# A hybrid decoder step on eight cores: the first two tiles taken block by block as weights land, and MLP weights converted to bf16 in a DRAM scratch

## The reference, cut to what matters

```python
h = rms_norm(x) * (1 + sc1) + sh1                    # shifts, scales and gates come from c @ w_ada + b_ada
q, fz, i, g, gb, gc, hv = split(h @ w_in)            # seven blocks of 512 columns
o_rec, s_rec_new = hgrn2_chunked(q, 1 - f, log(f), i, s_rec)      # f = lb + (1 - lb) * sigmoid(fz); state 4 x 128 x 128
o_rec = per_head_rms(o_rec) * g_onorm * silu(g)
y_conv, s_conv_new = short_conv(gc * hv, s_conv, w_conv)
x = x + g1 * (concat([o_rec, gb * y_conv]) @ w_out)
h2 = rms_norm(x) * (1 + sc2) + sh2
x = x + g2 * (square(relu(h2 @ w_up)) @ w_down)      # 1024 -> 4096 -> 1024
y = rms_norm(x) * g_final
```

## Time and profile before

| | us |
|---|---|
| median of three runs (1062.84 to 1077.37) | 1071.49 |
| the profiled execution | 1065.07 |
| its span on the slowest core, core 1 (all cores: 1051.7 to 1063.5) | 1063.5 |
| PE busy in the span | 837.0 (79%) |
| DVE / ACT / POOL busy | 476.9 / 341.9 / 213.9 |
| granted TensorE clock, mean of the slowest core | 0.953 |

### The profile page before, as it was taken

How to read it: one execution, slowest core, us unless ns; L and a number is a source line. 1 busy time by engine, 2 the same in 40 slices (tenths; PEclk the granted TensorE clock), 3 DMA queues, 4 the chain that set the end, 5 groups by cost and what they waited for, 6 DMA issues and landing times.

```text
span 1063.5 us, 16556 instructions; the slowest of 8 cores (1051.7 to 1063.5 us)
## 1 busy us (share of the span) xinstructions
PE 837.0 (79%) x5943; PEld 517.9 (49%) x5943; DVE 476.9 (45%) x953; ACT 341.9 (32%) x713; POOL 213.9 (20%) x248
## 2 busy tenths in 40 slices
PE   0100537999885898998707999999999999999996
PEld 0100336657664575675404645644654554564672
DVE  0000305778866877865605433452452452342331
ACT  2010303654463645554302413331431331230221
POOL 2010001244423442433411011001001001001101
PEclk9999968999997899999957999999999999999999
DMA  9999969232355333114999972112112101201100
GB/s 167 168 178 157 162 113 167 70 122 81 110 152 148 110 120 103 41 61 108 181 158 209 155 149 82 60 60 80 40 42 88 50 11 50 80 1 40 60 2 40
DMA packets 72415, 105.73 MB, mean 99 GB/s; under 512 B 3119, under 2 KB 58359, under 8 KB 72334
## 3 DMA queue, kind: packets, MB, share of 16 engines
q0 software_dynamic: 38624, 39.19, 27.1%
q1 hardware_dynamic: 33710, 65.48, 19.2%
HBM read 121.36 MB, written 22.49 MB: 135 GB/s over the span
## 4 chain that ended last, share of the span: by engine, by line
PE 59%; DMA 16%; DVE 10%; ACT 6%; issue 5%; another core or an unknown queue 2%; POOL 1%; DVEq 0%; POOLq 0%; ACTq 0%; SPq 0%
PE G L329 30%; PE U L329 20%; PE O L329 7%; DMA ada_116<-w_ada 7%; DMA adaf_106<-w_ada 4%; DMA wup_58<-w_up 4%; PE M L340 1%; DVE W_135 L373 1%; DVE h2T L369 1%; ACT WX_119 L356 1%; DVE Ts_83 L373 1%; ACT WX_118 L356 1%; ACT W_135 L356 1%; DVE W_137 L373 1%
## 5 line engine op out<-in xcount | busy, mean ns | idle before, releaser
L356 ACT ACTIVATE W_130<-xn_140 128x1024 bf16<-128x1024 f32 x13 | 13.7, 1052 | 144.2 <-PE M L340 132.1
L340 PE MATMUL M<-cB,W_129 128*128 128x128 bf16 (+1 forms) x144 | 12.9, 228 | 44.6 <-DVE W_129 L367 30.5
L329 PE MATMUL U<-ada_116,scT 128*17 128x512 bf16 x16 | 5.5, 504 | 48.5 <-DMA ada_116<-w_ada 48.5
L369 DVE TENSOR_SCALAR h2T<-M,modT 128x128 bf16<-128x128 bf16 x128 | 33.2, 333 | 14.7 <-PE M L340 14.7
L340 PEld LDWEIGHTS M<-cB,W_129 128*128 128x128 bf16 (+1 forms) x144 | 9.8, 103 | 47.0 <-issue 46.3
L356 ACT ACTIVATE W_129<-xn_139 128x1024 bf16<-128x1024 f32 x13 | 13.7, 1053 | 47.7 <-PE M L340 27.1
L356 ACT ACTIVATE W_134<-G 128x384 f32<-128x384 f32 (+2 forms) x36 | 18.1, 504 | 29.9 <-PE G L329 29.8
L329 PEld LDWEIGHTS U<-ada_116,scT 128*17 128x17 bf16 x16 | 1.6, 110 | 51.7 <-issue 50.9
L363 POOL TENSOR_TENSOR xr_142<-xr_142,W_133 128x512 f32<-128x512 f32 x7 | 9.6, 1369 | 81.2 <-DVE W_133 L363 80.6
L329 PE MATMUL U<-wout_50,mix_81 128*128 128x512 bf16 x80 | 19.6, 389 | 7.0 <-DVE mix_81 L363 5.9
L363 DVE TENSOR_TENSOR xr_141<-U,xr_141 17x512 f32<-17x512 f32 x2 | 1.4, 678 | 52.6 <-PE U L329 52.6
(11 more groups left out here) (569 smaller groups left out, 2236.9 us busy)
## 6 DMA issues: line engine op xcount, KB each, us to landing
xn_140<-x SPq DMA_DIRECT2D x9, 512.0 KB, 4.2
xn_139<-xp SPq DMA_DIRECT2D x8, 512.0 KB, 3.9
xn_140<-xp SPq DMA_DIRECT2D x8, 512.0 KB, 6.4
ada_116<-w_ada POOLq DMA_DIRECT2D x4, 1024.0 KB, 22.6
ada_117<-w_ada POOLq DMA_DIRECT2D x4, 1024.0 KB, 24.0
xn_139<-x SPq DMA_DIRECT2D x8, 512.0 KB, 4.4
xr_141<-xp SPq DMA_DIRECT2D x6, 512.0 KB
x<-xr_143 SPq DMA_DIRECT2D x6, 512.0 KB, 3.1
```

What stands on the lines that cost most here:

```text
L329: ins = e.matmul(o_, lhsT=l_, rhs=r_, start=st, stop=sp_, skip_group_check=True)
L340: ins = e.transpose(out=o_, in_=i_, identity=id_)
L356: return P.op("act", lambda e: e.activation(out=out, in_=in_, func=func, **kw), r, w, c, prio=prio)
L369: f = lambda e: e.tensor_scalar(out=out, in0=in0, scalar1=s1, scalar2=s2, op0=op0, op1=op1)
```

## The change

The first two tiles are put into the program together: for each of the seven blocks first the projection of tile 0, then that of tile 1 (`mixer_tile` becomes a generator that yields after each block). The two share weights as they land; `hT` gets a third buffer that lies in the place of `wout[1]`, so `load_out(1)` comes after the last projection of tile 1. `gates(0)` stays ahead of the tiles in the program, `mod_block` 6 to 9 move behind the fifth tile and `gates(1)` behind the sixth.

The MLP's weights are no longer loaded by POOL. Sixteen DMAs on POOL's queue (`convert`) read each 2.1 MB block in float32 and write it in bf16 to a DRAM scratch `wscr`, three per tile from the third tile on, each not before the 21st TensorE operation of its tile. `load_up` and `load_dn` then load 1.05 MB of bf16 each through SP, seven `load_up` being put ahead of the last tile's output projection, with the first group's `norm2`.

All weight inputs are rearranged on the host, so that a block is 128 rows of 16 KB in one piece; states and small vectors also come in the layout in which they are used, which removes the transposes and small DMAs that did it. `Sl` gets seven buffers, `mix` three, `kt` three, `sg` four; the key transposes move into the recurrence's loop; `normed` loads through ACT's DMA queue. In the scheduler the costs change, and on DVE and ACT an instruction now waits by semaphore for an earlier one of the same engine in all cases of overlap, not only where it reads what that one wrote.

```diff
-    DMA_BW = 310.0
+    SW_BW = 265.0
+    HW_BW = 150.0
...
-                            if d.eng == e and o.chan is None and (e == "pe" or (not raw and e != "pool")):
+                            if d.eng == e and o.chan is None and e == "pe":
                                 continue
...
+    wada_d = din("w_ada", [12, 128, 4096]); win_d = din("w_in", [7, 128, 4096]); wout_d = din("w_out", [2, 128, 4096])
+    wup_d = din("w_up", [8, 128, 4096]); wdn_d = din("w_down", [8, 128, 4096])
+    wscr_d = nc.dram_tensor("wscr", [16, 128, 4096], BF16, kind="Internal").ap()
...
+    hT.append(one("hT2", [128, 8, 256], BF16, offset=8 * 8192))
...
-    SlR = Ring("Sl", 4, [128, 512], F32, offset=u0)
+    SlR = Ring("Sl", 7, [128, 512], F32, offset=u0)
...
     def load_in(j):
-        dma("pool", win[j][:], wv(win_d, j * 512), [], [win_n[j]], MB2)
+        dma("pool", flat(win[j]), win_d[j], [], [win_n[j]], MB2)
...
+    def convert(i, after):
+        dma("pool", wscr_d[i], wup_d[i] if i < 8 else wdn_d[i - 8], [], ["wscr%d" % i], 1.5 * MB2, after=after)
 
     def load_up(j):
-        dma("pool", wup[j][:], wv(wup_d, j * 512), [], [wup_n[j]], MB2)
+        dma("sp", flat(wup[j]), wscr_d[j], ["wscr%d" % j], [wup_n[j]], MB2 / 2)
...
     def load_dn(j):
-        dh, a = j // 4, j % 4
-        dma("pool", wdn[j][:], wdn_v[a][:, :, dh * 512:(dh + 1) * 512], [], [wdn_n[j]], MB2)
+        dma("sp", flat(wdn[j]), wscr_d[8 + j], ["wscr%d" % (8 + j)], [wdn_n[j]], MB2 / 2)
...
         x, xn = xnR.take()
-        dma("sp", x[:], src_d, rdeps, [xn], 128 * 4096)
+        dma("act", x[:], src_d, rdeps, [xn], 128 * 4096)
...
+        yield "G"
+        mi = state["mixi"] % 3
...
-    hs[0] = norm1(*tiles[0])
+    CONV = list(UPORD) + list(range(8, 16))
+    hs[0] = norm1(*tiles[0]); hs[1] = norm1(*tiles[1])
     load_ada(4); load_ada(5)
-    for j in range(2):
-        load_out(j)
+    load_out(0)
     gates(0)
     load_gates(0)
-    for i, j in enumerate((6, 7, 8, 9)):
-        load_ada(j)
-        mod_block(j, i % 2 == 0, 24 + 8 * (i // 2), 16 + 8 * (i // 2))
-    load_ada(10); load_ada(11)
-    gates(1)
...
+    g0, g1 = gen(0), gen(1)
+    for step in ("F", "V", "Q", "G"):
+        assert next(g0) == step and next(g1) == step
+    next(g0); next(g1)
+    for step in ("C", "H", "B"):
+        assert next(g0) == step and next(g1) == step
+    load_out(1)
+    hs[2] = norm1(*tiles[2])
+    for g_ in (g0, g1):
+        for _ in g_:
+            pass
+    for n_ in range(2, len(tiles)):
+        t0op = len(P.ops)
         if n_ + 1 < len(tiles):
             hs[n_ + 1] = norm1(*tiles[n_ + 1])
+        for step in gen(n_):
+            if step == "B" and n_ + 1 == len(tiles):
+                WB = View(wall[2:6])
+                for j in UPORD[:7]:
+                    load_up(j)
+                norm2(bgroups[0])
+        mark = [o for o in P.ops[t0op:] if o.eng == "pe"][20:21]
+        if n_ == 4:
+            for i, j in enumerate((6, 7, 8, 9)):
+                load_ada(j)
+                mod_block(j, i % 2 == 0, 24 + 8 * (i // 2), 16 + 8 * (i // 2))
+        if n_ == 5:
+            load_ada(10); load_ada(11)
+            gates(1)
+        for _ in range(3):
+            if conv_i < 16:
+                convert(CONV[conv_i], mark)
+                conv_i += 1
-    for j in UPORD:
-        load_up(j)
+    load_up(7)
     load_gates(1)
     for j in range(8):
         load_dn(j)
...
+    blk = lambda w: np.ascontiguousarray(f(w).reshape(8, 128, -1, 512).transpose(2, 1, 0, 3).reshape(-1, 128, 4096))
```

More of the change, by code:

```diff
@@ L106, in op @@
         if dma is not None:
-            key = eng + ((":in:" + writes[0].name) if (writes and writes[0].rng is not None) else (":out:" + reads[0].name))
+            key = eng + ((":in:" + writes[0].name) if (writes and (writes[0].rng is not None or not reads)) else (":out:" + reads[0].name))
             o.chan = key
@@ L157, in schedule @@
             if o.dma is not None:
-                s = max(t + o.cost, dma_free)
-                dma_free = s + o.dma / self.DMA_BW
-                o.end = dma_free + 1900.0
+                sw = e == "pool"
+                s = max(t + o.cost, dma_free[sw])
+                dma_free[sw] = s + o.dma / (self.SW_BW if sw else self.HW_BW)
+                o.end = dma_free[sw] + 2500.0
             else:
@@ L167, in schedule @@
                 elif q.eng == e:
-                    x = o.end + (60.0 if (raw or e == "pool") and e != "pe" else 0.0)
+                    x = o.end + (60.0 if e != "pe" else 0.0)
                 else:
-                    x = o.end + self.LAT[e]
+                    x = o.end + self.LAT[e] + (self.PE_SLACK if q.eng == "pe" else 0.0)
                 if x > q.est:
@@ L386, in memset, with dma @@
         return P.op(eng, lambda e: e.memset(ap, val), [], w, 200.0)
-    def dma(eng, out, in_, r, w, nbytes, prio=None):
-        c = {"pool": 1000.0, "sp": 600.0, "act": 600.0}[eng]
-        return P.op(eng, lambda e: e.dma_start(out=out, in_=in_), r, w, c, dma=float(nbytes), prio=prio)
+    def dma(eng, out, in_, r, w, nbytes, prio=None, after=()):
+        c = {"pool": 1000.0, "sp": 600.0, "act": 100.0}[eng]
+        o = P.op(eng, lambda e: e.dma_start(out=out, in_=in_), r, w, c, dma=float(nbytes), prio=prio)
+        o.preds += [(d, True) for d in after]
+        return o
     at = {"p": 0}
@@ L451, in build_program, with mix_slot @@
     k0 = at["p"]
-    ktR = Ring("kt", 4, [128, 512], BF16)
+    ktR = Ring("kt", 3, [128, 512], BF16)
     vtR = Ring("vt", 4, [128, 512], BF16)
-    sgR = Ring("sg", 3, [128, 512])
+    sgR = Ring("sg", 4, [128, 512])
     mix = []
-    for i in range(2):
-        t, rg = place("mix%d" % i, [128, 8, 256], BF16)
+    def mix_slot(i, offset=None):
+        t, rg = place("mix%d" % i, [128, 8, 256], BF16, offset)
         for j in range(8):
@@ L704, in proj, with mixer_tile @@
         return bank, bn
[L706 removed]
+    def mixer_tile(kind, ti, last, h, hn, xblk):
         TT = 256 if kind == "p" else 128
@@ L759, in dn @@
             return [d[g][1] for g in range(len(groups))]
-        kt = []
-        for b in range(NB):
-            M, Mn = MR.take()
-            Mb = M[:, :].bitcast(BF16)
-            tr([(Mb[:, hd * 128:(hd + 1) * 128], hv(nk, hd, b * 128, (b + 1) * 128), ident) for hd in range(4)], dn(nk) + ["cB"], [Mn])
-            k_, kn = ktR.take()
-            copy("act", k_[:], Mb[:, 0:512], [Mn], [kn])
-            kt.append((k_, kn))
+        yield "Q"
         sg = {}
@@ L793, in mixer_tile @@
             v_, vn = vt[b]
-            k_, kn = kt[b]
+            M, Mn = MR.take()
+            Mb = M[:, :].bitcast(BF16)
+            tr([(Mb[:, hd * 128:(hd + 1) * 128], hv(nk, hd, t0, t0 + 128), ident) for hd in range(4)], dn(nk) + ["cB"], [Mn])
+            k_, kn = ktR.take()
+            copy("act", k_[:], Mb[:, 0:512], [Mn], [kn])
             M, Mn = MR.take()
@@ L1043, in build_program, with gen @@
-    for n_, (kind, ti) in enumerate(tiles):
+    bgroups = [[SAMPLE, 0, 1], [2, 3, 4], [5, 6, 7], [8, 9, 10], [11, 12, 13], [14, 15]]
+    conv_i = 0
+    def gen(n_):
+        kind, ti = tiles[n_]
+        return mixer_tile(kind, ti, kind == "p" and ti == 7, hs[n_][0], hs[n_][1], SAMPLE if kind == "s" else ti * 2)
+    g0, g1 = gen(0), gen(1)
[4 more added lines that the diff above has]
+        assert next(g0) == step and next(g1) == step
```

175 lines of the change are left out of this document (74 added, 101 removed).

## The result

The changed kernel takes 1032.17 us (median of 4), the kernel before, on the same chip, 1067.16: a ratio of 0.965 with a 95% interval from 0.957 to 0.973. It is faster by some 35 us, where 110 were forecast; 1032 lies above the range of 918 to 1010. Slow runs, such as one of 1069.16 us among these four, are left out of every ratio. The profiled execution has a span of 1031.9 us on core 5.

What follows compares the result with a forecast made beforehand. TensorE waits at the start for late weights and before the MLP behind POOL's queue; the MLP is full. Sum: 1065 - 89 - 6 + 8 + 10 + 10 - 10 + 3 - 36 = 955 us, range 918 to 1010.

Steps and rivals of the forecast that it cites:

- the conversions' cover: Mixer: idle DMA share hides sixteen conversions at 9 us each; 10 us charged for queueing, between 0 and 50.
- The ledger: Mixer from 149 us: existing DMA work 83, ada loads 43, conversions 144, together 270 of some 300 us.
- The -6: Start: fourteen long-row weight loads at 7.1 us instead of 7.5 gain 6 us; ends 20 gained, 7 lost.
- two output projections, 7: Start: the first two tiles' output projections together take 7 us, within the path reaching about 149 us.
- the gap of 36 us: Before the MLP: wait between last output projection and first up; removing it and slow matmuls gains 36, between 15 and 38.
- The +8 for moved products: Mixer: four mod_block and two gate products now run among the tiles, adding 8 us of TensorE.
- the +3 for DVE's waits on itself: Recurrence: about 285 more DVE instructions wait for their own engine, 26 us over the run, some 3 on the path.
- the sample tile's -10: Sample tile: seven buffers cut state rounds from four to three, gaining 10 us, between 0 and 15.
- The `ada` charge of 10: Mixer: waits for the second ada pair and for the state copy behind the following pair cost 10 us, between 4 and 30.
- (b): Mixer becomes DMA-bound from 10.9 us per conversion; at 14 us stretched by 50, POOL blocking Sb: 995 us, chance 0.15.
- (c): Conversions crawl, w_down comes late, slower than before; at 30 us per conversion about 1190 us, chance 0.07.
- (d): Start's recurrences hang on DVE and fixed order stalls in the mixer, 40 + 30 us lost: 1025 us, chance 0.08.

Runs made afterwards that it cites:

- 967 us kernel: 969 us kernel with w_down's loads issued behind the last tile's last addition and w_down's buffers placed as in the changed kernel: 966.7 us, ratio 0.911.
- that of 969: Changed kernel with only w_up's eight blocks converted, w_down loaded straight by POOL, ada pairs moved earlier, last state's store in another buffer ring: 969.0 us, 0.914.
- the dose of 7: Changed kernel, same order, with fifteen of sixteen conversions cut to 64 rows from 128: 980.4 us, 0.921; compared with cuts to 512 elements (0.925) and full conversions (0.965).
- 1: Changed kernel, same order, with fifteen of sixteen conversions writing only 512 elements and the MLP reading the one whole block: 984.0 us, ratio 0.925.
- 5: Changed kernel with the last state's product put in another ring's buffer, so no evacuation waits for its store: 1015.6 us, ratio 0.959.
- 4: Changed kernel with the planner counting 20 us to a hardware DMA's landing in the mixer and 12.5 for POOL's: 1013.9 us, ratio 0.957.

## Why the prediction was wrong

The step that failed is the one on the conversions' cover: "It fits, barely; loads and stores will queue. I charge 10 us for that, between 0 and 50." The ledger's price was met: conversions and `ada` loads were put at 16 x 9 + 43 = 187 us of all engines, and took 48.7% of 383, 187 us. That is a price under load, for the measured time holds what packets wait for each other: where only eight conversions run, the same count gives some 6.5 us for one in the 967 us kernel and 9 in that of 969. The ledger also left out the seven loads of `w_up` that the change puts ahead of the last output projection, 21 us at its own 3 us each. What was wrong is what a full ledger costs. 270 of 300 us is a share of 0.9, and the dose of 7 shows that a share of 0.67 is free and the step to 1 costs 47 us by the ratios. A load into `xn` that lands in 5 us at the one takes 12 to 25 at the other (medians), once 49, and each late landing holds all that stands behind it in its engine's queue, as the rows of SP, ACT and DVE above show. I had the mean share and took the mean for the risk. The term's own range reached to 50, and with 48 in place of 10 the sum is 993, inside the range of the whole: it took the start and the MLP as well to leave it.

Against the forecast the profiled span is 1031.9 - 953.4 = 78.5 us longer, and that parts as follows (places of the forecast: second tile done at 149.6 less the 6 for faster loads, so 143.6; first `up` 492.6 us ahead of the end, that is the earlier trace rows less 3 us of slow matmuls):
- The start: 161.9 - 143.6 = 18 us late. The -6 was not had: loads came sooner, but TensorE, busy 52.5 of 56 us, set the pace of the projections, and the recurrence began at 116, not 113. From there the terms held to the first output projection (142.9 against 142.6), though at a mean granted clock of 0.50 to 0.63 from 120 to 143 us (0.50 is the lower of its two levels, 1.2 GHz). What failed is "two output projections, 7": in the trace before one tile's alone takes 7, from 237.16 to 244.23, in four rows like this one.

```profile
237.16 1.89 PE L329 MATMUL U<-wout_50,mix_82 128*128 128x512 bf16 x8
```

  Two take 14 at that pace, and took 19 in the changed kernel (142.87 to 161.89), the first products at the lower clock and other products between.
- The mixer: 530.8 - 161.9 against 460.8 - 143.6, 52 us longer, with the 10 charged for the conversions counted in. 48 of its length go with the conversions (first `up` at 481.3 in 1, with a start 1.8 us earlier). So without them it is still some 14 longer than forecast without that charge; no run takes this apart. These are the slowest core's numbers: the eight cores have their first `up` product between 510 and 531 us.
- The MLP: 501.1 against 492.6, 8.5 us longer, for a wait that I did not see: the last state's store (27 us) holds the buffer that an evacuation wants, 10.1 us. With a buffer of its own (5) this part takes 493.2 us.

What held: the first projection (56 us, forecast 62); the first `up` directly behind the last output projection (529.07 + 1.89 against 530.80), so the gap of 36 us closed as described; a steady MLP (80.00 of 80). The +8 for moved products was not measured by itself, nor the +3 for DVE's waits on itself, nor the sample tile's -10. The `ada` charge of 10 (4 to 30) was 20.5 in the changed kernel and 9 without conversions, so the price was mostly that of the queue, not of the pair.

Of the rivals, (b) had the size, "50", by the wrong way: it began from 10.9 us per conversion, and they took some 9; and POOL was held by the rule of six for 3 us only. (c) did not happen. (d), "the fixed order stalls in the mixer", is near in time (1025) and in kind, but in 4 another order gives back only some 9 us of the loss while the share is near 1.

The tests named for a wrong forecast were the right ones: DMA shares near 1 through the mixer, and TensorE idle behind `ada`. The rule of the Trainium skill weighed there ("DMA: Bandwidth & Descriptors", "Issuing engines are not separate DMA queues": whoever issues them, transfers interleave on the same 16 engines) was borne out by `xn`, issued by ACT, that lands in 20.7 us beside POOL's conversions and in 4.7 without them.

## What to carry to other kernels

In these kernels background transfers were free while the DMA engines' share stayed at 0.67 to 0.74, and cost some 4% at 0.87 to 1.00. So compare the share with the work added in the stage where it runs, and where the sum comes near the full stage price the latency of every small transfer, not the bytes. Put into the background only what is wanted at once (here `w_up`, eight blocks of sixteen); what is wanted later can be loaded straight when it is due. Where engines work in order, look for what stands behind each transfer, above all small stores out of shared buffers: they become holes when transfers slow down, and closing one can move the wait on while the cause stays. Count a term from the rows before it goes into the sum: one tile's price had stood for two.

## What the runs showed of the hardware

- A casting DMA from DRAM to DRAM (2.1 MB read, 1.05 written, long rows) takes at best as much of the DMA engines as a casting load into SBUF, and more beside other work. POOL's queue, 37 blocks in all, took 237 us of them without conversions (23.8% of 993.9), so 6.4 a load; 237 and 258 with eight (24.6% of 965.4, 26.7% of 966.0), which leaves 6.5 to 9 for a conversion; and 283 with sixteen (27.4% of 1031.9), some 9.
- The same bytes in pieces of 512 elements take 205 us for 22 blocks. Pieces of 2048 elements were worst, with conversions that land after 67 us, though at a DMA share of only 0.67 in the window of 300 to 430 us: the share alone does not tell how long a transfer takes. That stays open.
- Casting loads in rows of 16 KB landed 6.8 us apart in the run of eight at the start, 7.9 in the first four; rows of 2 KB had 7.5.
- Beside weight loads a store of 256 KB held its buffer until 27 us after DVE wanted it, and one of 4 KB (`convp`) held POOL for 39.
- A hole costs its clock too: 0.67 and 0.63 were granted in the stretches with 14.40 of 40 and 7.56 of 33 us of work, where that from 162 to 205 us, with 41.65 of 43, has 1.00.
